# Reordering steps of a hand-written schedule, and moving two small start-up loads from ScalarE's queue to GpSimd's

## The chip, the cores and the metric

One core of a Trainium2 chip runs the whole program. The metric is the device time of one execution in microseconds (us); the kernel before was timed three times. A change of under 0.2%, about 2 us here, can't be told from no change.

## The reference, cut to what matters

Two layers of a hybrid decoder run over a prompt of 512 rows and over a sample group of 8 sequences with 8 new rows each (64 rows) and 2048 past positions.

```python
for l in range(DEPTH):                       # 2 layers; for the prompt rows, then for the sample rows
    h = rmsnorm(x, norm_pre[l]); z = h @ w_in[l]          # 1024 -> 3912 columns
    q, k, v, qi, ki, wi, ga, xb, gb, u, vc, gc = split(z)  # q, k, qi, ki get a partial rotation (rope)
    score = sum_h relu(qi . ki) * wi                      # indexer, causal
    idx = top_k(score)                                    # prompt 128 of 512, sample 256 of 2056
    ya = softmax(q . k[idx]) @ v[idx]                     # sample: keys and values of 16 pages of 128 and 8 new rows
    yb = (trailing window means of xb - xb) @ pool_w * pool_scale
    yc = u * (tril(sgu_w) @ layernorm(vc) + sgu_b)
    y = concat(ya * silu(ga), yb * silu(gb), yc * silu(gc))
    x = x + rmsnorm(y @ w_out[l], norm_post[l])
```

All is float32. The selection is computed as a mask: the kernel finds the threshold of the k-th score and adds minus infinity to what lies below it.

## The kernel before, in words

**Tiles.** The 576 rows are five row tiles: ST (the 64 sample rows) and 0 to 3 (128 prompt rows each). HT holds the normalised, transposed input; a projection step ("z", name, tile) multiplies one row tile by one 512-column chunk of w_in, 8 matmuls (L1573), for the ST tile in two column halves (L1547). A matmul of float32 appears twice in the trace's counts. "zk" is a part of such a step. The results lie in two PSUM banks that ScalarE empties (lines 905 to 931); three other banks are emptied by VectorE. A step that writes a bank waits until its last user is copied out.

**Order.** One list, written by hand in `_order()`, says what comes after what. Each engine's program runs through the same list and emits its own part of every step, so moving an entry moves work on TensorE (PE), ScalarE (ACT) and VectorE (DVE) at once. Both layers use the same list. `filler[m]` holds what is put around the heads 2m and 2m+1 of the prompt attention: its first part before the transposes of the previous pair's weights ("pt", L1932), its second part between those and the previous pair's product with V ("pv", L1831).

**Steps that the change touches.**
- ("snew", p): logits of the new sample keys (L1705). The first one waits for VectorE's copy of the transposed new keys, `pe.wait_ge(dve_free, dve_no(l, "kT", ST) + 1)`, the copy being L1264. Between them stands VectorE's bitwise search for the sample threshold ("sel", L1123 to L1156), then "take" (from L1162 on), which makes the mask.
- ("rope", "k", t), ("T", "kT", t): VectorE rotates the keys of tile t (L1114 to L1117), TensorE transposes them (L1586), VectorE copies them out (L1266). ("psel", a, b) is b - a rounds of VectorE's top-8 search in the prompt scores (L1131, L1134); 16 rounds are needed.
- ("K", p, j), ("V", p, j): TensorE runs over 8 pages of the cache (L1690, L1754), two sets of four. A page is 256 KB. SyncE (SP) issues the page loads (L724) into a ring of four groups of two pages, one group as soon as the one four back is used; so each K or V step uses up the ring, and each half of a step needs two groups. `group()` is the wait.
- ("turn", p, j): transposes of the sample weights (L1733), copied by ScalarE (L1020) for the V step. ("mask", p, n): mask spread (L1719, L1722) and added by VectorE (L1193). ("exp", p): ScalarE, L1011.
- ("pool", t), ("pool w", t): the pooling product (L1795, L1796), the gating product (L1802), then L1812. ("ln scale", t): four VectorE operations, L1324 to L1328. ("gaT", t), ("yT", t): transposes of the gate (L1943) and of the branches (L1950), VectorE's L1319 and L1479. ("qk", n): prompt logits, L1820, which VectorE masks (L1300).

**Start.** SyncE loads x_sample, the page table and the first prompt tile. ScalarE's queue loads the 128 x 128 identity and norm_pre (L944, L945), then, once the fourth part of the first weight chunk is in, the other three prompt tiles (L952). GpSimd (POOL) loads the first chunk of w_in in four parts (L759), the ki columns, the other constants (L798), and half of the indexer keys (L674); SyncE begins its half of the keys after the fourth weight part too. The first transposes (L1848) turn x into HT through L1237. `turn_x(0, 1)`, the transposes of prompt tile 0, stand after the first projection step.

Of the kernel before, what the change touches and what calls it, by code (L numbers as in the profile page):

```python
# [50 lines left out]
ST = PT_TILES  # L51
# [9 lines left out]
ROUNDS = KP // 8  # L61
# [32 lines left out]
CONST = {}  # L94
# [84 lines left out]
def _order():  # L179
    s = []  # L180

    def z(name, *tiles):
        s.extend(("z", name, rt) for rt in tiles)

    def rope(name, *tiles):
        s.extend(("rope", name, rt) for rt in tiles)

    def turned(name, *tiles):
        s.extend(("T", name, rt) for rt in tiles)
# [38 lines left out]
    for n in range(len(SI) + 1):  # L228
# [44 lines left out]
    s.append(("take",))  # L273
    z("v", 0)
    s.append(("snew", 0))
# [44 lines left out]
    z("gc", 0)  # L320
    rope("k", 2, 3)
    turned("kT", 1)
    s.append(("V", 1, 0))
    s += [("turn", 1, 1), ("psel", 9, 11)]
    z("gc", 1)
    turned("kT", 2)
# [4 lines left out]
        0: ([("z", "gc", 3), ("psel", 11, 13)], []),  # L331
        1: ([("z", "uv", ST), ("V", 1, 1), ("turn", 1, 2)], [("z", "uv", 0), ("K", 2, 3), ("psel", 13, 15)]),
        2: ([("zk", "uv", 1, 0, 4)], [("z", "uv", 1), ("V", 1, 2), ("turn", 1, 3), ("psel", 15, ROUNDS), ("pmask",)]),
# [7 lines left out]
        9: ([("gate", 1), ("snew", 3)], [("z", "ga", ST), ("K", 3, 3), ("pool", 1), ("yT", 0), ("pool w", 1), ("ln scale", 2)]),  # L341
        10: ([("ok", 0, 0, 4)], [("V", 2, 2), ("turn", 2, 3), ("gaT", 1), ("mask", 3, 0)]),
        11: ([("o", 0), ("ln scale", 3)], [("V", 2, 3), ("pool", 2), ("mask", 3, 1), ("turn", 2, 4), ("mask", 3, 2), ("exp", 3), ("pool w", 2)]),
# [16 lines left out]


ORDER = _order()


# [102 lines left out]
def build(nc, x_prompt, x_sample, k_pages_t, v_pages_n, kidx_t, state_pool, page_order, norm_pre_t, w_in, pool_w,  # L467
# [4 lines left out]
    with ExitStack() as ctx:  # L472
# [3 lines left out]
        def sem(name):  # L476
            return ctx.enter_context(nc.semaphore(name))
# [28 lines left out]
        V = vt[:, :].rearrange("p (t d) -> p t d", t=5)  # L506
# [43 lines left out]
        cst = sb("cst", consts.shape[1])  # L550
# [33 lines left out]
        gpre = sb("gpre", KC)  # L584
# [19 lines left out]
        gpre_first_in, gpre_in, gpost_in = sem("gpre_first_in"), sem("gpre_in"), sem("gpost_in")  # L604
# [36 lines left out]
        ident_in = sem("identity_in")  # L641
# [37 lines left out]
        n_id = CONST["ident"][1]  # L679
# [58 lines left out]
        def _(pool):  # L738
            def load_w(l, i, first=0, end=4):
# [8 lines left out]
                if i < len(CHUNKS):  # L748
                    _, c0, w = CHUNKS[i]
# [126 lines left out]
        def _(act):  # L876
# [67 lines left out]
            act.dma_start(cst[:, 0:n_id], consts[:, 0:n_id]).then_inc(ident_in, 16)  # L944
            act.dma_start(gpre[:, :], norm_pre_t[0]).then_inc(gpre_first_in, 16)  # L945
# [136 lines left out]
        def _(dve):  # L1082
# [275 lines left out]
            dve.wait_ge(gpre_first_in, 16)  # L1358
# [5 lines left out]
            for l in range(DEPTH):  # L1364
# [127 lines left out]
                for i, rt in enumerate(RTO):  # L1492
# [19 lines left out]
                    if l + 1 < DEPTH and i > 0:  # L1512
                        if i == 1:
                            dve.wait_ge(gpre_in, 16 * (l + 1))
                        if i <= 2:
                            copy_ht(l + 1, RTO[i - 1])
                        norm(l + 1, i - 1)
# [3 lines left out]
        def _(pe):  # L1521
# [356 lines left out]
            turn_x(0, 0)  # L1878
            for l in range(DEPTH):
                for s in ORDER:  # L1880
                    if s[0] == "x":
                        turn_x(l, s[1])
                    elif s[0] == "z":
                        project_tile(l, s[1], s[2], DONE_K.get(s[1:], 0))
                        if l == 0 and s == ORDER[0]:
                            turn_x(0, 1)
# [124 lines left out]
```

## Time and profile before

| | us |
|---|---|
| three runs | 1025.37, 1026.67, 1026.81 |
| median | 1026.67 |
| the profiled execution's own time | 1025.37 |
| its span in the trace | 1023.2 |
| PE busy | 985.8 |
| DVE busy | 564.3 |
| ACT busy | 297.1 |

The span is first to last instruction; 2.2 us of the execution lie around it. Layer 0 fills the time to about 510 us, layer 1 the rest. "Idle before" in a row is the time in which that engine did nothing ahead of the instruction, and the arrow names what released it. Some matmul records are missing, so not each hole between rows is a wait; a bracket with a releaser is.

### The profile page before, as it was taken

Reading aid. Unit: us, or ns where it says so; the run is one execution under the profiler, and the core shown is the slowest. Engines: PE = TensorE matmul, PEld = TensorE weight load, DVE = VectorE, ACT = ScalarE, POOL = GpSimd, SP = SyncE. Lnnn points to the kernel's source line nnn. Section 1 sums busy time; section 2 is a strip of 40 time slices with the busy share of each in tenths; the row PEclk is TensorE's granted clock in tenths of the full one; section 3 lists DMA queues with packets and bytes.
Section 4 is the critical chain, followed back from the end, with each engine's and each line's share of the span. In section 5 each row is a group of like instructions: output and inputs, shape, how many; then the busy total and the mean of one; then the engine's idle time right before and its main releaser. Section 6 shows DMA issues by size and latency. Waiting matters only on the chain.

```text
span 1023.2 us, 18691 instructions
## 1 busy us (share of the span) xinstructions
PE 985.8 (96%) x6442; PEld 503.0 (49%) x6442; DVE 564.3 (55%) x1733; ACT 297.1 (29%) x620; POOL 168.8 (16%) x290
## 2 busy tenths in 40 slices
PE   6999999999899999999999999999999999999994
PEld 4446444444654455555453644434456445555551
DVE  3327998566762345443541699955877324354332
ACT  2321111531331534232322211135123235323231
POOL 8450100110120000002725011010011200000000
PEclk9999999999999999999999999999999999899997
DMA  9382666466885666566542367674779666465521
GB/s 290 75 254 81 229 219 224 181 229 234 292 306 188 218 215 228 185 208 229 173 133 79 111 200 237 224 241 142 250 235 312 239 209 234 145 242 190 202 80 62
DMA packets 107391, 205.28 MB, mean 201 GB/s; under 512 B 15687, under 2 KB 24214, under 8 KB 107298
## 3 DMA queue, kind: packets, MB, share of 16 engines
q1 hardware_dynamic: 87474, 148.68, 42.4%
q0 software_dynamic: 19104, 53.77, 16.9%
q10 hardware_dynamic: 720, 1.64, 0.5%
q8 instruction: 52, 0.85, 0.4%
q14 instruction: 41, 0.34, 0.1%
HBM read 194.00 MB, written 10.14 MB: 200 GB/s over the span
## 4 chain that ended last, share of the span: by engine, by line
PE 89%; DVE 4%; DMA 2%; ACT 2%; SPq 1%; issue 1%; ACTq 0%; DVEq 0%; POOLq 0%
PE bank L1573 41%; PE bank L1871 11%; PE bank L1690 6%; PE bank L1754 6%; PE bank L1547 4%; PE bank L1820 3%; PE bank L1831 2%; PE bank L1906 2%; PE bank L1653 2%; PE bank L1669 2%; PE bank L1932 2%; PE bank L1866 1%; PE bank L1733 1%; DMA pg<-in_cache_v_dram 1%; PE bank L1586 1%; SPq L724 1%
## 5 line engine op out<-in xcount | busy, mean ns | idle before, releaser
L1573 PE MATMUL bank<-wr,ht 128*128 128x512 f32 (+1 forms) x1024 | 439.6, 576 | 3.7 <-ACT za L921 2.4
L1573 PEld LDWEIGHTS bank<-wr,ht 128*128 128x128 f32 x1024 | 187.3, 191 | 204.1 <-issue 194.7
L759 POOL DMA_DIRECT2D wr<-in_w_in_dram x64 | 46.6, 729 | 409.1 <-PE bank L1573 360.9
L1123 DVE TENSOR_SCALAR_CACHE_REDUCE r<-r,sel_i 128x1088 bf16<-128x1088 f32 x62 | 83.5, 1346 | 2.0
L674 POOL DMA_DIRECT2D pg<-in_cache_kidx_dram x128 | 67.0, 529 | 47.9 <-issue 42.1
L1754 PE MATMUL bank<-pg,rs 128*32 128x256 f32 x1024 | 64.2, 390 | 1.5 <-DMA pg<-in_cache_v_dram 1.0
L1690 PE MATMUL bank<-pg,r 128*32 128x256 f32 x1024 | 62.5, 382 | 1.1 <-DMA pg<-in_cache_k_dram 1.0
L759 POOL DMA_DIRECT2D wr<-in_w_out_dram x16 | 11.6, 726 | 294.2 <-PE bank L1871 132.7
L1547 PE MATMUL bank<-wr,ht 128*64 128x256 f32 (+1 forms) x512 | 58.2, 382 | 1.1 <-DMA wr<-in_w_in_dram 1.1
L1871 PE MATMUL bank<-wr,gr 128*128 128x512 f32 x128 | 58.5, 597 | 0.0
L1871 PE MATMUL bank<-wr,ht 128*128 128x512 f32 x128 | 58.3, 598 | 0.0
L1057 ACT ACTIVATE r<-r 128x128 f32<-128x128 f32 (+3 forms) x64 | 35.7, 559 | 63.4 <-DVE r L1303 63.2
L1134 DVE MATCH_REPLACE8 r<-r 128x256 f32<-128x256 f32 (+2 forms) x96 | 51.1, 543 | 0.0
L1300 DVE CUSTOM_DVE_ANT_0 r<-bank,r 128x256 f32<-128x256 f32 (+2 forms) x48 | 26.5, 553 | 42.9 <-PE bank L1820 42.9
L1690 PEld LDWEIGHTS bank<-pg,r 128*32 128x32 f32 x1024 | 29.9, 109 | 37.2 <-issue 18.5
L1754 PEld LDWEIGHTS bank<-pg,rs 128*32 128x32 f32 x1024 | 30.3, 111 | 36.0 <-issue 20.3
L1131 DVE MAX8 r<-r 128x8 f32<-128x256 f32 (+2 forms) x96 | 47.2, 547 | 0.6
L1547 PEld LDWEIGHTS bank<-wr,ht 128*64 128x64 f32 x512 | 35.9, 142 | 22.0 <-issue 6.5
L1020 ACT ACTIVATE rs<-bank 128x512 f32<-128x512 f32 (+1 forms) x40 | 21.1, 529 | 83.9 <-PE bank L1733 70.6
L1402 DVE COPY r<-bank 64x256 f32<-64x256 f32 x16 | 6.8, 422 | 63.0 <-PE bank L1669 62.9
L931 ACT ACTIVATE za<-bank,stats 128x512 f32<-128x512 f32 x16 | 11.0, 688 | 99.4 <-PE bank L1573 99.4
L1004 ACT ACTIVATE sh<-bank 128x512 f32<-128x512 f32 x32 | 19.1, 597 | 70.3 <-PE bank L1690 70.3
(256 smaller groups left out, 1235.3 us busy)
## 6 DMA issues: line engine op xcount, KB each, us to landing
pg<-in_cache_k_dram SPq DMA_DIRECT2D x256, 256.0 KB, 4.3
pg<-in_cache_v_dram SPq DMA_DIRECT2D x256, 256.0 KB, 4.5
wr<-in_w_in_dram POOLq DMA_DIRECT2D x56, 512.0 KB, 4.6
wr<-in_w_out_dram POOLq DMA_DIRECT2D x16, 512.0 KB, 4.5
pg<-in_cache_kidx_dram POOLq DMA_DIRECT2D x128, 32.0 KB, 2.3
pg<-in_cache_kidx_dram SPq DMA_DIRECT2D x128, 32.0 KB, 2.4
r<-in_x_prompt_dram SPq DMA_DIRECT2D x5, 512.0 KB, 6.2
out_dram<-vt POOLq DMA_DIRECT2D x8, 256.0 KB, 4.5
```

Source lines behind the costliest of these rows:

```text
L674: queue.dma_start(PG[2 * (g % 4) + e][par * HD:(par + 1) * HD, c0:c0 + PAGE], kidx_t[l, bass.ds(nos[u * 4 + par * 2 + f], 1), :, :].rearra ...
L759: pool.dma_start(W[n % 2][:, n4 * 2:n4 * 2 + 2, 0:w], src[:, n4 * 2:n4 * 2 + 2, :])\
L1057: nc.scalar.activation(SP_[n % 4][:, 0:w], SP_[n % 4][:, 0:w], ACT.Exp, bias=NB_[:, n:n + 1], scale=HD ** -0.5, accum_out=SM[:, n:n + 1]). ...
L1123: ins = nc.vector.tensor_scalar(junk[i][0:m, 0:part.shape[1]], part, sc, None, ALU.is_ge, ALU.add, accum_out=CNT[0:m, i:i + 1])
L1131: ins = nc.vector.max(BEST[:, i, :], part)
L1134: ins = nc.vector.match_replace(part, BEST[:, i, :], part, TAKEN)
L1547: mm = pe.matmul(b[t * NS:(t + 1) * NS, 0:w // 2], HT[:, k, SEQ:SEQ + NS], weights[:, k, t * (w // 2):(t + 1) * (w // 2)], start=(k == 0), ...
L1573: mm = pe.matmul(b[0:m, 0:w], HT[:, k, rt * P:rt * P + m], weights[k], start=(k == 0), stop=(k == KC - 1), skip_group_check=(k1 - k0 < KC))
L1690: mm = pe.matmul(bk[r0:r0 + HW, u * 256:(u + 1) * 256], QBX[:, 2 * e + k, q0:q0 + HW], two[par][:, :, 2 * e + k, :], start=(k == 0), stop= ...
L1754: mm = pe.matmul(acc[r0:r0 + HW, 0:DP], r[:, c0:c0 + HW], PG[s0[par] + e][:, g * DP:(g + 1) * DP], start=(j == 0 and u == 0 and e == 0), s ...
L1820: pe.matmul(b[:, 0:w], QT[part, h // 2, i * P:(i + 1) * P], KT[part, h // 2, 0:w], start=True, stop=True).then_inc(dve_full, 1)
L1871: mm = pe.matmul(b[0:m, :], y, W[n % 2][:, k, :], start=(i == 0), stop=(i == KC - 1), skip_group_check=(k1 - k0 < KC))
```

## The change

Two kinds of edits. First, `_order()` is altered in ten places, for both layers. Second, the identity and norm_pre loads go from ScalarE's program to the top of GpSimd's, ahead of the first weight chunk, norm_pre now counted on the semaphore that layer 1 also uses, and `turn_x(0, 1)` goes ahead of the first projection step.

```diff
     turned("kT", ST)
-    s.append(("take",))
+    s += [("take",), ("snew", 0)]
     z("v", 0)
-    s.append(("snew", 0))
...
     z("gc", 0)
+    s.append(("V", 1, 0))
+    s += [("turn", 1, 1), ("psel", 9, 11)]
     rope("k", 2, 3)
     turned("kT", 1)
-    s.append(("V", 1, 0))
-    s += [("turn", 1, 1), ("psel", 9, 11)]
     z("gc", 1)
+    s.append(("psel", 11, 12))
     turned("kT", 2)
...
-        0: ([("z", "gc", 3), ("psel", 11, 13)], []),
+        0: ([("z", "gc", 3), ("psel", 12, 14)], []),
...
-        9: ([("gate", 1), ("snew", 3)], [("z", "ga", ST), ("K", 3, 3), ("pool", 1), ("yT", 0), ("pool w", 1), ("ln scale", 2)]),
-        10: ([("ok", 0, 0, 4)], [("V", 2, 2), ("turn", 2, 3), ("gaT", 1), ("mask", 3, 0)]),
-        11: ([("o", 0), ("ln scale", 3)], [("V", 2, 3), ("pool", 2), ("mask", 3, 1), ("turn", 2, 4), ("mask", 3, 2), ("exp", 3), ("pool w", 2)]),
-        12: ([("V", 2, 4), ("od", 2), ("pool", 3)], [("turn", 3, 0), ("yT", 1), ("V", 3, 0), ("pool w", 3), ("ok", 1, 0, 4)]),
-        13: ([("turn", 3, 1), ("o", 1), ("V", 3, 1)], [("yT", 2), ("gate", 2), ("yTs",)]),
-        14: ([("turn", 3, 2)], [("gaT", 2), ("yo", 2), ("yT", 3)]),
-        15: ([("V", 3, 2), ("ok", 2, 0, 4)], [("turn", 3, 3), ("o", 2)]),
+        9: ([("gate", 1), ("snew", 3)], [("K", 3, 3), ("z", "ga", ST), ("pool", 1), ("yT", 0), ("pool w", 1), ("ln scale", 2)]),
+        10: ([("ok", 0, 0, 4)], [("V", 2, 2), ("turn", 2, 3), ("gaT", 1), ("ln scale", 3), ("mask", 3, 0)]),
+        11: ([("o", 0)], [("pool", 2), ("mask", 3, 1), ("V", 2, 3), ("turn", 2, 4), ("mask", 3, 2), ("exp", 3), ("pool w", 2)]),
+        12: ([("V", 2, 4), ("od", 2), ("pool", 3)], [("turn", 3, 0), ("yT", 1), ("pool w", 3), ("V", 3, 0), ("ok", 1, 0, 4)]),
+        13: ([("turn", 3, 1), ("o", 1), ("V", 3, 1), ("yT", 2)], [("gate", 2), ("yTs",)]),
+        14: ([("turn", 3, 2)], [("gaT", 2), ("yo", 2), ("yT", 3), ("V", 3, 2)]),
+        15: ([("ok", 2, 0, 4)], [("turn", 3, 3), ("o", 2)]),
...
         def _(pool):
+            n_id = CONST["ident"][1]
+            pool.dma_start(cst[:, 0:n_id], consts[:, 0:n_id]).then_inc(ident_in, 16)
+            pool.dma_start(gpre[:, :], norm_pre_t[0]).then_inc(gpre_in, 16)
...
-            act.dma_start(cst[:, 0:n_id], consts[:, 0:n_id]).then_inc(ident_in, 16)
-            act.dma_start(gpre[:, :], norm_pre_t[0]).then_inc(gpre_first_in, 16)
...
             turn_x(0, 0)
+            turn_x(0, 1)
             for l in range(DEPTH):
...
-                        if l == 0 and s == ORDER[0]:
-                            turn_x(0, 1)
```

In filler 1 and 2 the last psel rounds go from 13 to 15 and 15 to 16 to 14 to 16 in filler 1 alone; in filler 4 ("K", 3, 0) goes ahead of ("mask", 2, 1). In the new file the lines after 735 stand mostly one to three lower.

TensorE around the first "snew", before: the transposes of the new keys, the v projection of tile 0, then the new keys' logits (small, r), and the next projection part.

```order
L1586 MATMUL bank<-cst,zb 128x64 x4
L1573 MATMUL bank<-wr,ht 128x512 x8
L1705 MATMUL bank<-small,r 32x64 x8
L1573 MATMUL bank<-wr,ht 128x512 x4
L1690 MATMUL bank<-pg,r 32x256 x16
```

The same place in the changed kernel.

```order
L1587 MATMUL bank<-cst,zb 128x64 x4
L1706 MATMUL bank<-small,r 32x64 x8
L1574 MATMUL bank<-wr,ht 128x512 x12
L1691 MATMUL bank<-pg,r 32x256 x16
L1574 MATMUL bank<-wr,ht 128x512 x2
```

The logits now stand directly behind the transposes.

TensorE from the gc projection of the ST tile on, before: the gc projection of tile 0, the transposes of key tile 1 (cst, zb), V step (1, 0) (pg, rs), the weight transposes (cst, sh), gc of tile 1, key tile 2, gc of tile 2, K step (2, 2).

```order
L1547 MATMUL bank<-wr,ht 64x128 x16
L1573 MATMUL bank<-wr,ht 128x256 x8
L1586 MATMUL bank<-cst,zb 128x128 x4
L1754 MATMUL bank<-pg,rs 32x256 x16
L1733 MATMUL bank<-cst,sh 128x128 x4
L1573 MATMUL bank<-wr,ht 128x256 x8
L1586 MATMUL bank<-cst,zb 128x128 x4
L1573 MATMUL bank<-wr,ht 128x256 x8
L1690 MATMUL bank<-pg,r 32x256 x16
```

The same place in the changed kernel.

```order
L1548 MATMUL bank<-wr,ht 64x128 x16
L1574 MATMUL bank<-wr,ht 128x256 x8
L1755 MATMUL bank<-pg,rs 32x256 x16
L1734 MATMUL bank<-cst,sh 128x128 x4
L1587 MATMUL bank<-cst,zb 128x128 x4
L1574 MATMUL bank<-wr,ht 128x256 x8
L1587 MATMUL bank<-cst,zb 128x128 x4
L1574 MATMUL bank<-wr,ht 128x256 x8
L1691 MATMUL bank<-pg,r 32x256 x16
```

The V step and the weight transposes moved ahead of key tile 1. On VectorE two psel rounds now stand between the rotation of key tile 1 and those of tiles 2 and 3, and one round between the copies of key tiles 1 and 2.

TensorE around V step (3, 2), before: the end of the product of a head pair with V (r or pt, vt), the logits of the next pair (kt, qt), the V step, the first part of output tile 2.

```order
L1831 MATMUL bank<-r,vt 64x128
L1831 MATMUL bank<-pt,vt 64x128
L1820 MATMUL bank<-kt,qt 128x512 x2
L1754 MATMUL bank<-pg,rs 32x256 x16
L1871 MATMUL bank<-wr,ht 128x512 x4
```

The same V step in the changed kernel, from the transposes of "yT" 3 (cst, gr) on.

```order
L1950 MATMUL bank<-cst,gr 128x128 x4
L1755 MATMUL bank<-pg,rs 32x256 x16
L1832 MATMUL bank<-r,vt 64x128
L1832 MATMUL bank<-pt,vt 64x128
L1832 MATMUL bank<-r,vt 64x128
```

It now comes ahead of the whole product of the head pair and of the next logits.

## Rows read from the trace of the kernel before

**Rows 1.** Page, part 1: busy us, share, instructions.

```profile
PE 985.8 (96%) x6442; PEld 503.0 (49%) x6442; DVE 564.3 (55%) x1733; ACT 297.1 (29%) x620; POOL 168.8 (16%) x290
```

**Rows 2.** Waits of TensorE: engine line <- releaser: us, times, longest.

```profile
PE bank L1586 <- DVE zb L1117: 4.3, 2, 2.2
...
PE bank L1812 <- DVE sst L1193: 1.8, 2, 0.9
...
PE bank L1690 <- DMA pg<-in_cache_k_dram: 1.0, 1, 1.0
...
PE bank L1722 <- DVE zb L1343: 1.0, 2, 0.5
```

**Rows 3.** Timeline, PE, start: us, duration, what.

```profile
7.13 6.46 PE L1547 MATMUL bank<-wr,ht 128*64 128x256 f32 x32 [1.13 <-DMA wr<-in_w_in_dram]
13.52 1.09 PE L1848 MATMUL bank<-cst,r 128*128 128x128 f32 x8
14.54 1.21 PE L1573 MATMUL bank<-zb,ht 128*64 128x72 f32 x16
18.13 3.70 PE L1573 MATMUL bank<-wr,ht 128*128 128x512 f32 x8 [2.37 <-ACT za L921]
```

**Rows 4.** Timeline, start, other engines.

```profile
6.64 0.56 POOL L798 DMA_DIRECT2D cst<-in_consts_dram  x1
...
7.52 1.06 ACT L940 ACTIVATE gr<-r 128x1024 f32<-128x1024 f32 x1 [0.76 <-DMA r<-in_x_prompt_dram]
...
15.60 1.41 ACTq L952 DMA_DIRECT2D r<-in_x_prompt_dram  x3
```

**Rows 5.** DMA issues, 0 to 22 us: issuer, KB, us to landing.

```profile
cst<-in_consts_dram ACTq DMA_DIRECT2D x1, 64.0 KB, 2.3
```

**Rows 6.** Timeline, PE and DVE, around the first "snew".

```profile
161.10 7.13 PE L1573 MATMUL bank<-wr,ht 128*128 128x512 f32 x16
163.06 0.42 DVE L1264 COPY small<-bank 128x256 f32<-128x256 f32 x1
169.01 0.70 PE L1573 MATMUL bank<-wr,ht 128*128 128x512 f32 x1 [0.40 <-ACT vt L931]
```

**Rows 7.** Timeline, DVE, a psel round, a key copy, a rotation's end.

```profile
260.78 1.48 DVE L1131 MAX8 r<-r 128x8 f32<-128x256 f32 x3
...
264.00 0.69 DVE L1266 COPY kt<-bank 128x512 f32<-128x512 f32 x1
...
266.24 0.29 DVE L1117 TENSOR_TENSOR zb<-zb,plt 128x128 f32<-128x128 f32 x1
```

**Rows 8.** Timeline, DVE, mask and "ln scale" of tile 3.

```profile
405.67 0.68 DVE L1193 CUSTOM_DVE_ANT_0 sh<-sh,bank 128x512 f32<-128x512 f32 x1
...
408.21 0.15 DVE L1324 RECIPROCAL stats<-stats 128x1 f32<-128x1 f32 x1
...
409.19 0.42 DVE L1328 TENSOR_TENSOR gr<-gr,pscale 128x256 f32<-128x256 f32 x1
```

**Rows 9.** Pages of V step (3, 2): issues, us to landing.

```profile
L724 SPq DMA_DIRECT2D pg<-in_cache_v_dram x8: 333/333/1162, 438.8 to 443.6; - x8
...
DMA to landing us min/median/max: 4.7/5.8/6.3
```

**Rows 10.** Chain that ended last, 438 to 452 us: start, us, what.

```profile
440.73 0.69 DVE r L1471
...
441.46 1.09 PE bank L1831 x16
...
447.26 1.02 PE bank L1831 x16
448.28 1.06 PE bank L1820 x4
449.34 1.86 PE bank L1754 x32
```

**Rows 11.** Stretch: length, PE DVE ACT POOL busy, PEclk, DMA share, GB/s.

```profile
764.10:767.50 3.40, 3.40 (x33) 1.57 (x25) 3.33 (x10) 0.00 (x0) 0.00 (x0) 0.55 0.59 193
```

More of the change, by code:

```diff
@@ L330, in _order @@
     filler = {
-        0: ([("z", "gc", 3), ("psel", 11, 13)], []),
-        1: ([("z", "uv", ST), ("V", 1, 1), ("turn", 1, 2)], [("z", "uv", 0), ("K", 2, 3), ("psel", 13, 15)]),
-        2: ([("zk", "uv", 1, 0, 4)], [("z", "uv", 1), ("V", 1, 2), ("turn", 1, 3), ("psel", 15, ROUNDS), ("pmask",)]),
+        0: ([("z", "gc", 3), ("psel", 12, 14)], []),
+        1: ([("z", "uv", ST), ("V", 1, 1), ("turn", 1, 2)], [("z", "uv", 0), ("K", 2, 3), ("psel", 14, ROUNDS)]),
[1 row of a table added]
         3: ([("snew", 2), ("yo", 0), ("zk", "uv", 2, 0, 4)], [("z", "uv", 2), ("V", 1, 3), ("turn", 1, 4)]),
[1 row of a table removed]
[1 row of a table added]
         5: ([("z", "ga", 0)], [("K", 3, 1), ("turn", 2, 0)]),
@@ L603, in build @@
         small_in, table_in = sem("small_in"), sem("table_in")
-        gpre_first_in, gpre_in, gpost_in = sem("gpre_first_in"), sem("gpre_in"), sem("gpost_in")
+        gpre_in, gpost_in = sem("gpre_in"), sem("gpost_in")
         wt_ready = sem("gating_weights_ready")
@@ L678, in build @@
         block = ctx.enter_context(nc.Block())
-        n_id = CONST["ident"][1]
         @block.sync
@@ L1357, in _ @@
             dve.wait_ge(init_done, 1)
-            dve.wait_ge(gpre_first_in, 16)
+            dve.wait_ge(gpre_in, 16)
             for i in range(2):
@@ L1513, in _ @@
                         if i == 1:
-                            dve.wait_ge(gpre_in, 16 * (l + 1))
+                            dve.wait_ge(gpre_in, 16 * (l + 2))
                         if i <= 2:
```

3 rows, old and new, of the table filler are left out of this document.

## The prediction

> **What bounds the kernel now.** I read the page first, then TensorE's waits, then the timelines around each place that the change touches, and for the page loads the landing times. TensorE is busy for 985.8 of 1023.2 us and no other engine for more than 564 [rows 1], so the time is TensorE's queue from end to end, and an edit counts only by what it puts into or takes out of TensorE's waits. These are few and each is small: 4.3 us for the rotated keys (two waits, one a layer), 1.8 and 1.0 us for VectorE ahead of the last mask and of L1812, 1.0 us once for cache pages [rows 2], some microseconds at the start [rows 3]. All the change can gain lies in those; what it can lose is set by how close the other engines stand behind. The work of TensorE itself is not changed by one matmul.
>
> **The start.** The first projection runs from 7.13 to 13.6 us, the transposes of prompt tile 0 take 1.09 behind it, the ki projection 1.2, and then TensorE waits 2.37 us until 18.13 for ScalarE to empty the first bank [rows 3]. ScalarE is late because it first finishes the norm of tile 0, which hangs on those transposes, and then issues three loads for 1.41 us from 15.60 on [rows 4]. With the transposes in front, the norm is long done. The tile is in at 7.5 us [rows 4]; transposes to 8.6, the projection of 6.46 to 15.1, its two copies end at 16.1, the ki projection at 16.3, where tile 0's projection can start: 1.8 us earlier than 18.13. The loads in GpSimd's queue put the weights back by two issues of 0.56 each [rows 4], 1.1 us, which the later start of the projection (8.6 for 7.1) hides. The identity took 2.3 us on ScalarE's queue [rows 5] and now goes through a queue on which no small first load is shown; if it takes 2.3 there too it lands at about 3.7, under the 4.9 at which x_sample lets the first transposes go. Bounds: -2.6 if the projection, which ran at 0.20 us a record here against half of that later in the trace, speeds up where it did, and +0.9 if the identity comes as late as the first weight part did (7.1), which pushes all behind it. I take -1.8, once.
>
> The Trainium skill (DMA: Bandwidth & Descriptors, Specifications and Issuing engine by pattern) speaks against this part: plain loads belong on the sync or scalar queue, with a first byte after about 0.6 us against about 1 us from GpSimd. By that the identity would come 0.4 us later than it did, and the start would still be bound by x_sample. The trace of before has no like pair of loads to check it.
>
> **The first "snew".** TensorE has the new keys transposed at 161.1 and goes into the v projection until 168.2; VectorE copies those keys only at 163.06 to 163.48, because its threshold search stands in front [rows 6]. Nothing in the change moves VectorE's work there, and its chain up to there has no wait for TensorE in it since 92.8 us, so the distance stays. Put directly behind the transposes, the logits wait from 161.15 to 163.5: +2.35 us, and the whole of TensorE's queue waits behind them. Later the projection part behind them need no longer wait 0.40 for ScalarE [rows 6]. Net +1.95 a layer, +3.9 in all. Layer 1 has the same order and the same distance. Bounds +1.5 and +2.1 a layer; below that nothing can go, since the instructions on both engines are the same.
>
> **Key tiles, V step (1, 0) and psel.** The wait of 2.16 us a layer [rows 2] is for the rotation of tile 1, which stands on VectorE behind two psel rounds. The V step and the weight transposes now fill it. But tile 2's rotation comes behind two more rounds. A round is 260.78 to 264.00, 3.2 us; the rotations of tiles 1 and 2 lie between 264.6 and 266.5, 0.95 each [rows 7]. So tile 2 is rotated 2 x 3.2 + 0.95 = 7.35 after tile 1 (at 265.6), at 273.0, and its transposes, which began at 272.2, wait for it: +0.8. What the V step now waits for its own pages, being 2.6 us earlier, ends under this wait. The page wait of 1.0 at the following K step in layer 0 [rows 2] goes, its pages being asked for earlier: -0.4 there with the small parts. In layer 1 TensorE ran V step (1, 0) at half clock [rows 11], 1.6 us that the new wait covers: -0.9. Sum -1.3. Bounds: -5.3 (the wait gone in both layers, and the page wait) and +2.
>
> **"ln scale" 3, "pool" 2, V (2, 3).** VectorE's four operations, 408.21 to 409.61, are put ahead of the mask work at 405.67 [rows 8]. The second of the logits behind needs the bank that the first mask operation frees, now 1.4 later: +1.3. Against it the V step stands between the mask products and what waits for them, and the waits of 0.9 and 0.5 a layer [rows 2] go: -1.4. Net -0.1 in both layers together; bounds -2.8 and +2.6.
>
> **"yT" 2 ahead of the weights' transposes.** The head product at 441.46 waits for VectorE's copies of the transposed weights, the last begun at 440.73 [rows 10]. Ahead of the two now stands one more copy of 0.6: +0.6 a layer, +1.2. Bounds 0 and +1.4.
>
> **V step (3, 2).** It moves ahead of a head product and two logits, 1.02 and 1.06, from 449.34 to 447.2 [rows 10]. Its last two pages are issued up to 443.6 and take 5.8 to land in the median [rows 9]: 449.4. The second half needs them at 448.1, and waits 1.35. What lies behind, head product and output projection, needs as long as before. +2.7 for two layers; bounds 0 (landing after the 4.7 of the quickest) and +3.6 (after the 6.3).
>
> **The rest** (K (3, 3) and K (3, 0) earlier, L1812 ahead of V (3, 0), psel in fillers 1 and 2) exchanges neighbours on TensorE whose inputs are ready by the trace, and costs nothing; K (3, 3), 3.6 us earlier, uses up its margin on pages: 0 to +0.7.
>
> **Sum.** -1.8 + 3.9 - 1.3 - 0.1 + 1.2 + 2.7 = +4.6 us on the profiled execution's 1025.37 (span 1023.2, 2.2 around it). It lies 1.3 under the median of 1026.67; the difference is carried over, which gives 1031.3 us.
>
> **Rivals.**
> (B) The page waits don't come and the start gives its best. For it: landing varies between 4.7 and 6.3 [rows 9]. Against it: the ring allows no earlier issue. 4.6 - 2.7 - 0.8 = +1.1, 1027.8, no change that can be told.
> (C) The clock decides, on the faster side. In 764.1 to 767.5 the granted clock was 0.55 [rows 11], half of 2.4 GHz; just before, TensorE had stood for 2.16 us for tile 1's rotation. By the same view two more such stretches lie at 419.4 (3.4 us) and 869.9 (6.9 us), the first behind the waits for the last mask. Together 13.7 us at half speed, 6.8 lost. If the clock no longer falls once those waits are filled, 5.9 more than I counted come back, and the 1.3 by which the median is above the profiled run too: 1024.1. It decides once three of these falls are gone. Against it: the change makes new waits of 2.35 and 2.
> (D) The reverse: the four new waits (two at "snew", two at tile 2) each bring one such stretch of 3.4 us, 1.7 lost in each: +6.8, 1038. For it: the wait of 2.16 did so in one layer. Against it: in the other it did not.
>
> **Chances.** Forecast 0.56, B 0.19, C 0.13, D 0.12. What can be told from no change is 0.2%, 2.05 us. Slower 0.68 (forecast and D), same 0.19, faster 0.13. The forecast's own range is 1028.7 to 1034; the range that holds 8 in 10 reaches into B and D and the unknown clock: 1025.8 to 1035.5.
>
> **What would show it.** In the changed profile: the new keys' logits begin about 2.3 us behind the transposes, released by VectorE's copy, in both layers; tile 0's first projection part at about 16.3; key tile 2's transposes wait about 2 us for the rotation; a wait for cache_v pages of about 1.4 in V step (3, 2); no waits ahead of the last mask and L1812, but 1.3 at the logits before. It is wrong if the logits find the keys copied, if the V step finds its pages, or if the granted clock falls at other places than before for more than 3 us in all.

## The result, and the profile after

| | before | changed |
|---|---|---|
| first timing, median of 6 runs each | 1026.74 | 1036.53 |
| ratio, 95% interval | | 1.0099 [1.0076, 1.0121] |
| second timing (that of e9 below), median of 27 and 12 runs | 1028.73 | 1033.30 |
| ratio, 95% interval | | 1.0038 [1.0016, 1.0061] |
| profiled execution, its own time | 1025.37 | 1030.69 |
| its span, mean granted clock | 1023.2, 0.988 | 1029.0, 0.994 |

The changed kernel is slower: +9.8 us in the first timing, +4.6 in the second. 1031.3 was forecast from 1026.7, with 1025.8 to 1035.5 as the range. The sign was right, and the first measurement lies outside.

One measure is used below beside the time. The granted clock of TensorE differs from execution to execution: in 125 runs of the kernel before its mean lay anywhere between 0.977 and 0.994, and those runs spread from 1023 to 1036 us. (One further run of it and one each of e7 and e15, over 1.5% above the fastest of their kernels, are left out everywhere.) A "fall" below is a stretch in which the granted clock stands at half. It costs half its length where TensorE is the limit, so **span times mean granted clock** follows what the execution would take without falls ("at equal clock"). Its mean was 1012.5 to 1012.9 for the kernel before in each of the four batches of timings, and it tells single edits apart better than the time does.

Two things in it are not the cost of falls. First, each profile also ends at half clock, with TensorE's last matmul long done; in the kernel before no engine is busy there (columns: stretch, length, busy us of PE, PEld, DVE, ACT, POOL with counts, granted clock, DMA share, GB/s):

```profile
1013.00:1023.20 10.20, 0.00 (x0) 0.00 (x0) 0.00 (x0) 0.00 (x0) 0.00 (x0) 0.50 0.13 50
```

This end lasted 9.0 to 12.2 us in the seventeen profiles, so it takes 4.5 to 6.1 us off each product and cancels in a difference only to about 1 us. Second, 1.7 us of a timed execution lie around the span where the two loads are moved, and 2.1 elsewhere. Taken of the whole time, such a kernel is 0.4 better than the column "equal clock" below says: e1 -1.9, e14 +0.8, e9 +7.7, e10 +4.5, e11 -2.2, e12 -4.5.

The two profiles differ by 5.8 us in span (5.3 in time), but the kernel before lost 6.8 us to three falls of the clock ahead of its end and the changed one 1.7 to this one (columns as above):

```profile
910.70:914.10 3.40, 3.40 (x6) 1.28 (x5) 1.36 (x8) 1.42 (x4) 0.00 (x0) 0.51 0.71 244
```

With these falls taken out, the changed profile is 10.9 us longer.

TensorE's work is the same; part 1 of the changed kernel's page, against [rows 1], is 2.4 us less busy; less of it ran at half clock:

```profile
PE 983.4 (96%) x6442; PEld 502.6 (49%) x6442; DVE 563.8 (55%) x1733; ACT 297.2 (29%) x620; POOL 169.2 (16%) x292
```

The waits of TensorE in the changed kernel, against [rows 2]:

```profile
PE bank L1755 <- DMA pg<-in_cache_v_dram: 6.8, 10, 1.3
PE bank L1706 <- DVE small L1265: 4.7, 2, 2.4
...
PE bank L1587 <- DVE zb L1118: 3.8, 2, 2.0
PE bank L1821 <- DVE sst L1194: 2.8, 4, 1.0
PE bank L1832 <- DVE r L1472: 1.4, 2, 0.7
...
PE bank L1813 <- DVE r L1472: 0.8, 2, 0.5
...
PE bank L1691 <- DMA pg<-in_cache_k_dram: 0.7, 1, 0.7
```

The waits ahead of the last mask and of L1812 are gone as forecast, and so is the one for ScalarE at the start. New are the one for the new keys (4.7), ten waits for V pages where there were two of 1.0 in all, four for VectorE's mask operation, two at the head product and two at a pooling product.

A wait printed there is not all that was lost: a group whose instructions wait for one another shows its first wait and grows longer. So each instruction of TensorE was set against the same one of the kernel before (the n-th of its line and tiles), and the shift read at both ends of each edit's place. The ledger of these shifts, in us, has the falls of the clock taken out. It is that of one pair of executions:

| place | forecast | layer 0 | layer 1 |
|---|---|---|---|
| start | -1.8 | -2.6 | |
| first snew | +3.9 | +1.9 | +1.9 |
| V (1, 0), psel, key tiles | -1.3 (+0.4 without the clock) | -0.3 | +1.2 |
| K (3, 0) ahead of mask (2, 1) | 0 | +1.1 | +1.1 |
| K (3, 3) ahead of ga | 0 to +0.7 | +0.8 | 0 |
| ln scale 3, pool 2, V (2, 3) | -0.1 | -0.2 | -0.1 |
| pool w 3 ahead of V (3, 0) | 0 | +0.9 | +1.2 |
| yT 2 ahead of pt | +1.2 | +0.7 | +0.7 |
| V (3, 2) | +2.7 | +0.9 | +1.6 |

The rows sum to 10.8; page waits at other places, up to 0.6 each and of both signs, nearly cancel. Two rows that were forecast at nothing, K (3, 0) and pool w 3, make 4.3 of it.

**Start.** TensorE in the changed kernel, against [rows 3]. Columns: start, duration, engine, line, what, idle before and its releaser.

```profile
4.69 1.11 PE L1849 MATMUL bank<-cst,r 64*128 64x64 f32 x8 [4.69 <-DMA cst<-in_consts_dram]
6.80 1.97 PE L1849 MATMUL bank<-cst,r 128*128 128x128 f32 x8 [1.00 <-DMA r<-in_x_prompt_dram]
8.71 5.79 PE L1548 MATMUL bank<-wr,ht 128*64 128x256 f32 x32
14.33 1.16 PE L1574 MATMUL bank<-zb,ht 128*64 128x72 f32 x16
15.55 3.70 PE L1574 MATMUL bank<-wr,ht 128*128 128x512 f32 x8
```

Tile 0's projection starts at 15.55 for 18.13. The identity's load was issued later (at 1.40 for 0.88) and took 3.3 us for the 2.3 of [rows 5], so it landed at about 4.7 and not at the 3.7 of the prediction. It now is what the first transposes wait for; they start no later, since x_sample had held them until 4.91. On GpSimd's slower first byte the Trainium skill (DMA: Bandwidth & Descriptors, Specifications) and the trace agree in the direction: the page has about 1 us against about 0.6, and here the same load took 1.0 us more from issue to landing.

**First snew.** As forecast, in both layers:

```profile
158.14 0.46 PE L1587 MATMUL bank<-cst,zb 64*128 64x64 f32 x4
160.94 0.45 PE L1706 MATMUL bank<-small,r 128*32 128x64 f32 x16 [2.34 <-DVE small L1265]
161.31 8.85 PE L1574 MATMUL bank<-wr,ht 128*128 128x512 f32 x20
```

**V step (1, 0) and the key tiles.** Layer 0:

```profile
263.33 1.07 PE L1755 MATMUL bank<-pg,rs 128*32 128x256 f32 x16
265.56 1.07 PE L1755 MATMUL bank<-pg,rs 128*32 128x256 f32 x16 [1.16 <-DMA pg<-in_cache_v_dram]
266.56 0.66 PE L1734 MATMUL bank<-cst,sh 128*128 128x128 f32 x4
267.05 0.60 PE L1587 MATMUL bank<-cst,zb 128*128 128x128 f32 x4
267.49 3.62 PE L1574 MATMUL bank<-wr,ht 128*128 128x256 f32 x16
272.93 0.63 PE L1587 MATMUL bank<-cst,zb 128*128 128x128 f32 x4 [1.82 <-DVE zb L1118]
```

The key wait of 2.16 is gone. In its place are 1.16 for pages in the V step and 1.82 for the rotation of tile 2.

**K (3, 0) ahead of mask (2, 1).** First the kernel before, then the changed one: the mask product and the K step in their two orders (in the second only the end of the K step), and the logits of the next head pair.

```profile
331.00 0.40 PE L1719 MATMUL bank<-r,repb 64*128 64x256 bf16 x4
331.33 1.93 PE L1690 MATMUL bank<-pg,r 128*32 128x256 f32 x32
...
333.69 0.70 PE L1820 MATMUL bank<-kt,qt 64*128 64x256 f32 x4
```

```profile
331.75 1.05 PE L1691 MATMUL bank<-pg,r 128*32 128x256 f32 x16
332.73 0.40 PE L1720 MATMUL bank<-r,repb 64*128 64x256 bf16 x4
...
333.91 1.30 PE L1821 MATMUL bank<-kt,qt 64*128 64x256 f32 x4 [0.39 <-DVE sst L1194]
```

The mask product now stands behind the K step, so VectorE adds the mask, and frees the bank, later. Its first mask operation, before and then changed:

```profile
331.43 0.69 DVE L1193 CUSTOM_DVE_ANT_0 sh<-sh,bank 128x512 f32<-128x512 f32 x1 [2.85 <-PE bank L1719]
```

```profile
333.16 0.69 DVE L1194 CUSTOM_DVE_ANT_0 sh<-sh,bank 128x512 f32<-128x512 f32 x1 [4.72 <-PE bank L1723]
```

The logits wait 0.39 at their start and lengthen from 0.70 to 1.30, about 1 us in all, in both layers.

**pool w 3 and V (3, 0)**, and then **the head product behind yT 2** and **V (3, 2)**, all in layer 0:

```profile
426.05 0.68 PE L1813 MATMUL bank<-pw,plt 128*128 128x128 f32 x4 [0.36 <-DVE r L1472]
426.66 1.07 PE L1755 MATMUL bank<-pg,rs 128*32 128x256 f32 x16
428.18 1.07 PE L1755 MATMUL bank<-pg,rs 128*32 128x256 f32 x16 [0.45 <-DMA pg<-in_cache_v_dram]
...
443.20 0.32 PE L1832 MATMUL bank<-kip,vt 128*64 128x128 f32 x1 [0.71 <-DVE r L1472]
...
448.92 1.07 PE L1755 MATMUL bank<-pg,rs 128*32 128x256 f32 x16
450.70 1.07 PE L1755 MATMUL bank<-pg,rs 128*32 128x256 f32 x16 [0.72 <-DMA pg<-in_cache_v_dram]
```

### The profile page after: what moved, and what is told of

It reads as the page before. It is cut to its first block, busy times and chain, and to the rows that moved or that the text cites. A ratio compares the mean times of both kernels' runs of the same rounds, so it can differ in the third digit from the quotient of the medians.

```text
span 1029.0 us, 18691 instructions
## 1 busy us (share of the span) xinstructions
PE 983.4 (96%) x6442; PEld 502.6 (49%) x6442; DVE 563.8 (55%) x1733; ACT 297.2 (29%) x620; POOL 169.2 (16%) x292
## 4 chain that ended last, share of the span: by engine, by line
PE 69%; DVE 18%; DMA 6%; SPq 3%; issue 2%; ACT 2%; DVEq 0%
PE bank L1574 29%; PE bank L1872 11%; DVE r L1124 8%; DMA pg<-in_cache_v_dram 5%; PE bank L1755 4%; PE bank L1691 3%; SPq L723 3%; PE bank L1548 3%; PE bank L1821 2%; PE bank L1654 2%; PE bank L1670 2%; PE bank L1906 2%; DVE sel_i L1155 2%; PE bank L1832 1%; PE bank L1867 1%
## 5 line engine op out<-in xcount | busy, mean ns | idle before, releaser
L1429 DVE SCALAR_TENSOR_TENSOR r<-rs,wi,r 128x256 f32<-128x256 f32 (+2 forms) x42 | 26.0, 618 | 24.0 <-ACT rs L998 21.5
```

## The experiments

Fifteen kernels, in four batches, each batch on one chip beside 27 to 35 runs of the kernel before. "Median" is that of the timed runs (12, where no other number stands), "equal clock" the difference to the kernel before in mean span times clock with its 95% interval, "clock" the mean granted clock (that of the kernel before behind it). Kernels of one batch are set against the same runs of the kernel before, so they share its error: e1 to e4, e5 to e8, e9 to e12, e13 to e15.

| | median / before | ratio [95%] | equal clock | clock / before |
|---|---|---|---|---|
| e1 start | 1026.6 / 1029.9 | 0.9969 [0.9948, 0.9989] | -1.5 ± 1.8 | 0.987 / 0.985 |
| e2 snew | 1036.5 / 1029.9 | 1.0058 [1.0031, 1.0084] | +3.6 ± 1.4 | 0.982 / 0.985 |
| e3 keys | 1028.6 / 1029.9 | 0.9972 [0.9943, 1.0002] | -1.5 ± 1.3 | 0.985 / 0.985 |
| e4 mask | 1029.3 / 1029.9 | 1.0008 [0.9980, 1.0035] | +1.7 ± 1.4 | 0.987 / 0.985 |
| e5 lnpool | 1028.7 / 1029.9 | 0.9993 [0.9967, 1.0018] | +2.1 ± 1.5 | 0.988 / 0.985 |
| e6 poolw | 1028.3 / 1029.9 | 0.9982 [0.9959, 1.0006] | +1.8 ± 1.3 | 0.988 / 0.985 |
| e7 yT 2 (11 runs) | 1027.8 / 1029.9 | 0.9976 [0.9947, 1.0006] | +2.0 ± 1.3 | 0.989 / 0.985 |
| e8 V (3, 2) | 1032.1 / 1029.9 | 1.0015 [0.9988, 1.0042] | +3.1 ± 1.2 | 0.986 / 0.985 |
| e9 changed, again | 1033.3 / 1028.7 | 1.0038 [1.0016, 1.0061] | +8.1 ± 1.2 | 0.989 / 0.985 |
| e10 no snew | 1028.3 / 1028.7 | 0.9986 [0.9962, 1.0010] | +4.9 ± 1.3 | 0.991 / 0.985 |
| e11 start, keys (10 runs) | 1022.1 / 1028.7 | 0.9939 [0.9916, 0.9963] | -1.8 ± 1.0 | 0.990 / 0.985 |
| e12 start, V first (6 runs) | 1020.2 / 1028.7 | 0.9898 [0.9867, 0.9929] | -4.1 ± 1.4 | 0.991 / 0.985 |
| e13 transposes | 1025.6 / 1028.0 | 0.9975 [0.9954, 0.9997] | -2.7 ± 1.4 | 0.987 / 0.987 |
| e14 loads | 1028.9 / 1028.0 | 1.0016 [0.9988, 1.0043] | +1.2 ± 1.6 | 0.987 / 0.987 |
| e15 K (3, 3) (11 runs) | 1030.7 / 1028.0 | 0.9998 [0.9973, 1.0023] | -0.6 ± 1.5 | 0.986 / 0.987 |

**e1, the start alone, and its halves e13 and e14.** e1 makes the edits of the change at L944, L945 and at `turn_x`; e13 moves `turn_x(0, 1)` alone, e14 the loads alone.

```diff
+            turn_x(0, 1)
-                        if l == 0 and s == ORDER[0]:
-                            turn_x(0, 1)
+            pool.dma_start(cst[:, 0:n_id], consts[:, 0:n_id]).then_inc(ident_in, 16)
+            pool.dma_start(gpre[:, :], norm_pre_t[0]).then_inc(gpre_in, 16)
```

> The kernel before with the start of the changed one alone (identity and norm_pre through GpSimd's queue, tile 0's transposes ahead of the first projection). Theory A (an edit costs the waits at its own place, the granted clock takes no side): the first projection part of tile 0 begins at about 15.6 us for 18.13, and all of it is kept to the end: -2.6 us. Theory B (the timed loss of 9.8 us, 4.5 more than between the two profiled executions, comes from more falls of the clock): also about -2.6 here, since no wait is added. Theory C (what TensorE gains it gives back at the cache pages, which do not come earlier): -1.2 or less, with new page waits of 0.4 or more in layer 0.

> The kernel before with the transposes of prompt tile 0 alone ahead of the first projection; identity and norm_pre stay on ScalarE's queue. A: all of the start's gain is in the transposes, tile 0's first projection part begins 1.5 to 2.5 us earlier than 18.13, -2 us by time multiplied by clock. Forecast of the start: -1.8, of which this is all. Rival: the transposes are only worth something with the loads moved, 0 to -0.5.

> The kernel before with the identity and norm_pre loads alone moved to GpSimd's queue ahead of the first weight chunk. A: the weights come two issues of 0.56 us later and the first projection with them, +1.1 us; ScalarE, free earlier, doesn't change the wait for the first bank. Rival: 0 or a small gain, since the first projection also waits for the transposes of x_sample, whose identity comes no later.

The start is 3.3 us faster in the times and 1.5 at equal clock; the halves give -2.7 and +1.2 (of the whole time -2.7 and +0.8, e1 -1.9), which add up to it. The transposes carry the gain. What the moved loads do is inside the noise, and by e14's trace it is small: TensorE begins the first projection at 7.62 (7.13 before) and tile 0's projection at 18.44 (18.13 before), and the wait for ScalarE stands as it was. Behind it is a fall of the clock, read off the duration: 5.40 us for the eight products that take 3.70 in [rows 3].

```profile
7.62 6.09 PE L1548 MATMUL bank<-wr,ht 128*64 128x256 f32 x32 [1.81 <-DMA wr<-in_w_in_dram]
...
18.44 5.40 PE L1574 MATMUL bank<-wr,ht 128*128 128x512 f32 x8 [2.57 <-ACT za L924]
```

In e13 the same part has no wait and its full speed:

```profile
8.75 1.97 PE L1848 MATMUL bank<-cst,r 128*128 128x128 f32 x8 [2.46 <-DMA r<-in_x_prompt_dram]
10.65 5.17 PE L1547 MATMUL bank<-wr,ht 128*64 128x256 f32 x32
15.65 1.16 PE L1573 MATMUL bank<-zb,ht 128*64 128x72 f32 x16
16.88 3.70 PE L1573 MATMUL bank<-wr,ht 128*128 128x512 f32 x8
```

Of the ten profiled kernels with that wait nine show this fall (the kernel before, in the execution of [rows 3], is the tenth), of the seven without it none. e1's profile also speaks against theory C: the K step's page wait of 1.0 in layer 0 was 0.2, and two V steps waited 2.0 together. The intervals don't part A from C (-2.6 from -1.2).

**e2, the first snew alone.**

```diff
-    s.append(("take",))
+    s += [("take",), ("snew", 0)]
     z("v", 0)
-    s.append(("snew", 0))
```

> The kernel before with the first snew alone directly behind the transposes of the new keys. A: +1.95 a layer less small change behind, +3.7 us in all. B: as A, and a fall of the clock of 3.4 us behind each of the two waits, +7.1. C: the later page steps find their pages sooner, so that of the 1.95 of each layer less than 1 is left, +2 or less.

+3.6 at equal clock, theory A's number, and +6.6 in the times, close to B's. Both are right: the wait costs what was forecast, and the times add the clock. Theory C's 2 lies below the interval of the 3.6. The fall behind it comes in some executions only: of the six snew waits in the profiles of e2, the changed kernel and e9, three have it. e9's, with the wait just ahead (columns as above; the stretch behind the wait, then the one that holds it):

```profile
163.50:167.00 3.50, 3.50 (x5) 1.35 (x4) 3.42 (x5) 0.05 (x1) 0.00 (x0) 0.52 1.03 386
160.00:163.50 3.50, 1.12 (x25) 0.86 (x22) 3.30 (x9) 0.77 (x2) 0.00 (x0) 1.00 0.95 304
```

**e3, V step (1, 0) and psel ahead of the key tiles, alone.** The edit is that of the change at `rope("k", 2, 3)`, with the three fillers' psel numbers.

> The kernel before with V step (1, 0), its weight transposes and the psel rounds alone ahead of key tiles 1 to 3. A: per layer 2.16 gone, 1.8 to 2.0 new at key tile 2, 1.0 to 1.2 new for pages in the V step; in layer 0 the 1.0 at K step (2, 2) goes: +1 us in all at equal clock. B: +1, and less 1.7 if the fall of the clock behind the old wait in layer 1 goes. What was forecast for this edit: -1.3.

```profile
267.15 1.07 PE L1755 MATMUL bank<-pg,rs 128*32 128x256 f32 x16 [1.16 <-DMA pg<-in_cache_v_dram]
...
274.52 0.63 PE L1587 MATMUL bank<-cst,zb 128*128 128x128 f32 x4 [1.82 <-DVE zb L1118]
```

The two new waits are those of the changed kernel to a hundredth, as theory A has it, yet the sum is -1.5 ± 1.3 and not +1. One thing that A had too small is the page wait at K step (2, 2). It was 1.0 in the kernel before, once; over the eleven profiled kernels that lack this edit it came in 8 of 22 layers, 0.2 to 3.3 us, 15.6 in all, which is 1.4 an execution. In the five kernels with the edit it came in none of 10. One profile shows such a wait at one of its values, not at its mean. This moves A's +1 to about +0.6 only, and the rest of the difference isn't explained. From e11 less e1 the edit comes out at -0.3 ± 2 instead.

**e4, K step (3, 0) ahead of mask (2, 1).**

```diff
-        ... ("mask", 2, 1), ("K", 3, 0), ("od", 1), ...
+        ... ("K", 3, 0), ("mask", 2, 1), ("od", 1), ...
```

> The kernel before with K step (3, 0) alone ahead of the second mask part of group 2. A: the logits of the next head pair wait for the bank that VectorE frees later, as the changed kernel's trace has it: +1.05 us a layer, +2.1 in all. Forecast: nothing (neighbours with ready inputs). B: as A, with no further fall, since the wait is short.

+1.7 ± 1.4 at equal clock, with A's +2.1 inside and the forecast's 0 just outside; no clear change in the time. The trace has the wait and the stretched logits exactly as in the changed kernel, in both layers:

```profile
336.68 1.30 PE L1820 MATMUL bank<-kt,qt 64*128 64x256 f32 x4 [0.39 <-DVE sst L1193]
```

**e5, ln scale 3 and pool 2 alone.** The edits of the change in fillers 10 and 11.

> The kernel before with ln scale 3 alone ahead of the last masks, and pool 2 and the second mask product ahead of V step (2, 3). Theory A (waits at the place, as the changed kernel's trace has them): +1.4 a layer at the logits behind, -1.4 a layer at the two waits that V step (2, 3) now covers, 0 in all. Theory B (clock): the falls of the clock at about 419 and 870 to 920 stood behind those two waits; without the waits they are gone and 1.7 to 3.4 us come back. Theory C (pages): V step (2, 3), now later, finds its pages and V step (2, 4) behind it does not: +0.5 to +1.

+2.1 ± 1.5 at equal clock, nothing in the time. The profile has +1.3 and -1.4 at the two places, as theory A says; what stands beside that is a page wait of 3.3 at K step (2, 2), which is 130 us ahead of the edit and not its doing. Theory B is half right: the fall at 419 is gone, and the one in layer 1 came all the same at 915, behind the new wait of 1.0 at the logits. The interval leaves out theory A's 0, but the trace has no cost at the place, so whether the edit costs anything is left open by this run.

**e6, pool w 3 ahead of V step (3, 0).**

```diff
-        12: (..., ("V", 3, 0), ("pool w", 3), ("ok", 1, 0, 4)]),
+        12: (..., ("pool w", 3), ("V", 3, 0), ("ok", 1, 0, 4)]),
```

> The kernel before with pool w 3 alone ahead of V step (3, 0). A: the last pooling product now waits 0.4 for VectorE's copy (L1471), and V step (3, 0) behind it, being no later than before against its pages, 0.4 to 0.7 in its second half: +0.9 to +1.2 a layer, +2 in all. Forecast: nothing. C: the V step waits for its pages wherever it stands, so that only the 0.4 counts, +0.8.

+1.8 ± 1.3 at equal clock. Here the V step found its pages and only the pooling product waited:

```profile
431.41 0.68 PE L1812 MATMUL bank<-pw,plt 128*128 128x128 f32 x4 [0.36 <-DVE r L1471]
432.02 1.93 PE L1754 MATMUL bank<-pg,rs 128*32 128x256 f32 x32
```

By the trace the edit alone costs 0.4 to 0.5 a layer, which is C's +0.8; the interval holds both C's and A's number. The page wait of 0.45 and 0.73 that the changed kernel's profile has at this V step came neither here nor in the profiles of e9 and e10, which have the edit together with its neighbours. It is one execution's, and not a cost that the edit always brings.

**e7, yT 2 alone.** `("yT", 2)` at the end of filler 13's first part.

> The kernel before with yT 2 alone ahead of the transposes of the weights. A and forecast: the head product behind waits 0.6 to 0.7 more for VectorE's copies, +1.3 in all. C: V step (3, 2) behind it, which is later by that, finds its pages as before; nothing is given back, +1.3 too. Rival: the 0.7 is hidden at the output projection, 0.

The head product waits 0.7 in each layer, and +2.0 ± 1.3 holds the 1.3 expected. The rival's 0 lies outside.

**e8, V step (3, 2) alone.** `("V", 3, 2)` from the head of filler 15 to the end of filler 14.

> The kernel before with V step (3, 2) alone moved ahead of the head product. A and forecast: its second half waits 1.0 to 1.5 for its pages in each layer, +2 to +3 in all. Rival: landing nearer to the quickest 4.7 us, the wait is under 0.5 a layer: +1 or less. B: two more waits of over 1 us, each with a fall of the clock of 3.4 us behind it: +5.5.

+3.1 ± 1.2 at equal clock: the forecast of 2.7 holds. In layer 1 the step waited 0.70 for pages and nothing fell behind it, so B is half right at most. In layer 0 it waited 0.45 and 1.53, and the second half runs at half clock (1.94 for 1.07), the clock having fallen behind the wait:

```profile
456.13 1.07 PE L1754 MATMUL bank<-pg,rs 128*32 128x256 f32 x16 [0.45 <-DMA pg<-in_cache_v_dram]
458.73 1.94 PE L1754 MATMUL bank<-pg,rs 128*32 128x256 f32 x16 [1.53 <-DMA pg<-in_cache_v_dram]
```

**e15, K step (3, 3) alone.**

```diff
-        9: (..., [("z", "ga", ST), ("K", 3, 3), ...
+        9: (..., [("K", 3, 3), ("z", "ga", ST), ...
```

> The kernel before with K step (3, 3) alone ahead of the ga projection of the sample tile. A: its second half waits 0.6 to 0.8 us for pages in one layer or both, +0.7 to +1.5 by time multiplied by clock. Forecast: 0 to +0.7. Rival: its margin of 3.3 us on the pages covers the 3.6 it moves, 0.

-0.6 ± 1.5, and no page wait at the step in either layer: the rival holds. The changed kernel waited 0.66 there in layer 0, e9 and e10 0.40 each, so the wait seems to need the other edits.

**e9, the changed kernel again, and e10, the same without the snew edit.**

> The changed kernel again, beside runs of the kernel before on the same chip, so that it can be set against the single edits. Theory A (the loss is the sum of the waits of its edits): time multiplied by the granted clock lies 9 to 10 us above the kernel before, the sum of the eight single edits by that measure being 10.2. Rival (the edits disturb each other): it lies above by 13 or more, or by less than 7. Clock as in the kernel before within 0.002.

> The changed kernel with the first snew alone put back behind the v projection of tile 0. A: 3.5 to 3.9 us faster than the changed kernel. B (clock): 6 to 7 faster, as its single edit cost in the times. C (pages): with TensorE 1.9 a layer earlier, page waits grow by 0.5 to 1 a layer, and only 2 to 2.5 come back.

At equal clock the changed kernel is 8.1 ± 1.2 above the kernel before; the nine single edits sum to 10.7, with an interval of about ± 4. The 8.1 is below the 9 to 10 of theory A and above the 7 of the rival, with both just inside the interval; no disturbance of one edit by another is needed, and none is excluded. The expectation for the clock (within 0.002 of the kernel before) was missed: it was 0.989 for 0.985, 3.4 us of 1030, and so the times show only +4.6. Without snew 3.2 ± 1.3 come back at equal clock and 5.0 in the medians: theory A's wait, and the clock on top. C's 2 to 2.5 lies inside that interval too, but the page waits of e10's profile are not longer than those of e9's (4.2 and 0.6 us for V and K pages, against 5.7 and 0.4).

**e11, the start and the key edit together, and e12, a version of our own.** e12 takes the start, and moves V step (1, 0) ahead of key tile 1 as the change does, but leaves the rotations ahead of the psel rounds:

```diff
     rope("k", 2, 3)
+    s += [("V", 1, 0), ("turn", 1, 1)]
     turned("kT", 1)
-    s.append(("V", 1, 0))
-    s += [("turn", 1, 1), ("psel", 9, 11)]
+    s.append(("psel", 9, 11))
     z("gc", 1)
```

> The kernel before with two edits of the change alone: the start, and V step (1, 0) with the psel rounds ahead of the key tiles. A: the sum of the two singles, -2.8 us by time multiplied by clock, faster than both kernels. C (pages give it back): -1.3, the start alone.

> The kernel before with the start of the changed one, and V step (1, 0) and its weight transposes put ahead of the transposes of key tile 1, but with the rotations of key tiles 2 and 3 left ahead of the psel rounds. A: the wait of 2.16 us a layer is filled, 1.2 a layer comes new for pages in the V step, the 1.9 a layer at key tile 2 does not come, and the page wait at K step (2, 2) goes: 1.9 a layer better than start_keys, -5 to -6 us against the kernel before. Rival (the transposes of key tile 1, now later, hold up its copy and with it the logits): no better than start_keys.

Both beat both kernels. e11's -1.8 ± 1.0 at equal clock holds A's -2.8 and C's -1.3 alike; the rest of its 6.6 us in the medians is a clock of 0.990 for 0.985. e12 is at 0.9898 [0.9867, 0.9929] of the kernel before, 8.5 us, of which 4.1 ± 1.4 at equal clock, for the 5 to 6 expected. Its timeline shows the page wait in the V step and none at the key tiles:

```profile
261.12 1.07 PE L1755 MATMUL bank<-pg,rs 128*32 128x256 f32 x16
263.44 1.07 PE L1755 MATMUL bank<-pg,rs 128*32 128x256 f32 x16 [1.26 <-DMA pg<-in_cache_v_dram]
...
264.94 0.60 PE L1587 MATMUL bank<-cst,zb 128*128 128x128 f32 x4
265.38 3.62 PE L1574 MATMUL bank<-wr,ht 128*128 128x256 f32 x16
268.83 0.60 PE L1587 MATMUL bank<-cst,zb 128*128 128x128 f32 x4
```

It is 2.3 ± 1.7 better than e11 at equal clock, where 3.8 was expected. K step (2, 2) in layer 1 had its page wait again (1.5), so the key edit's other gain may be partly lost here.

## Why the prediction was wrong

**Right, in mechanism and size.** The snew wait (+3.9 forecast, +3.7 in the ledger, +3.6 in e2), ln scale and pool 2 in the ledger (-0.1, -0.3), yT 2 (+1.2, +1.4), V (3, 2) (+2.7, +2.5; e8 +3.1). The start has the right mechanism and was set too small: -1.8 for -2.6. The prompt tile was in at 6.8 and not at 7.5; the transposes took 1.97 us for the 1.09 I took, but the projection behind them 5.79 for 6.46. The sum also kept 2.2 us around the span, which is 1.7 in the changed kernel.

**The step that failed** is "the rest exchanges neighbours on TensorE whose inputs are ready by the trace, and costs nothing". K (3, 0) lost nothing itself, but the mask product that it passed came 1.7 us later (332.73 for 331.00), VectorE's mask work with it, and the logits behind need the bank which that work frees: 2.2 in both layers together, with the same wait of 0.39 a layer in the profiles of e4, e9 and e10. I had asked this question of ln scale 3, where the answer was right, and not here. For pool w 3 the input was in fact not ready: VectorE's copy had been covered by the 1.93 of the V step in front, and came 0.36 and 0.46 late without it, 0.8, in every profile with the edit. The other 1.2 of that row are page waits of the V step behind, which the profiles of e9 and e10 don't have. So the step that was put at nothing costs 3 us each time, and 4.3 in the profiled execution; e4 and e6 together have +3.5 at equal clock.

**The key edit** was nearly right by its waits: tile 2's transposes forecast at 273.0 and measured at 272.93, in a kernel that stood 0.2 us earlier just ahead of the place. Up to there +0.8 a layer was forecast, and the shifts are +0.9 in layer 0 and +1.2 in layer 1; in layer 0 the page wait at K step (2, 2) goes, as forecast, which makes the -0.3 of the ledger. That wait was counted at the one value that one profile showed; its mean is 1.4 an execution for that 1.0. By e3 the edit is even a gain, -1.5 ± 1.3; by e11 less e1 it is -0.3 ± 2.

**The clock.** Rivals C and D were both true in part. Old waits had falls behind them: at the start 9 of 10, at key tile 1 14 of 22 over all profiled kernels. New waits have them too: snew 3 of 6, key tile 2 2 of 10. A third pair is the largest: the old waits of 0.49 and 0.88 us ahead of the last mask and of L1812 had a fall behind them in 19 of 26 layers, four of these falls 13.7 us long, and the wait of 1.01 at the logits, which took their place, in 5 of 8. By these shares and lengths, an estimate, the old waits cost an execution 7.8 us of clock and the new ones 5.0. The change takes away more falls than it adds, and so the second timing gives it back 3.4 us of its 8.1. The forecast of +4.6 agrees with that second timing (+4.6), and this is no merit: it had 6.2 at equal clock (4.6 and the 1.6 that it took back from the clock at V step (1, 0)) instead of 8 to 11, and 1.6 of clock given back instead of 3.4. Two errors offset.

**What stays open.** Why the first timing shows 9.8 and the second 4.6: the intervals, 1.0076 to 1.0121 and 1.0016 to 1.0061, don't meet. At equal clock the changed kernel was 1021.9 in the first and 1020.9 in the second, and its mean clock was 0.987 and 0.989, so 2 of the 3.2 us by which its own time differs are clock. The other 2.0 of the 5.2 lie with the kernel before, whose clock in the six runs of the first timing isn't known except for one (0.988). That it was granted a better clock there is likely, not shown. Nor is it shown why key tile 2's wait of 1.6 to 2.5 us brings a fall so much more seldom than key tile 1's 2.16 or the shorter waits ahead of L1812.

## What to carry to other kernels

When a step is moved, ask of each step that it passes what that one releases, and follow this to the next bank or buffer in demand: K (3, 0) cost 2.2 us that way with none of its own inputs late. Where two waits stand one behind the other on the same engine, put work into the first without delaying what ends the second: e12, with the rotations left in front, is 2.3 ± 1.7 us at equal clock better than e11, which has the change's own order there. Weigh small edits by a measure that the clock hardly moves (span times granted clock), and read a page wait over several executions before it is counted as a gain or a loss.

## What the runs showed of the hardware

A wait of TensorE of 2.2 to 2.7 us can cost more than itself: behind it the granted clock falls to half, mostly for 3.4 us, 1.7 more. The fall comes at the same wait in one execution and not in another: 9 of 10, 14 of 22, 3 of 6, 2 of 10 at the four places with waits of about 2 us. The length of the wait doesn't decide it: waits of 0.49 and 0.88 us in a row had one in 19 of 26 layers, and four of these falls lasted 13.7 us, 6.8 lost. This is e8's (the columns of the clock rows above):

```profile
421.30:434.90 13.60, 13.31 (x82) 9.41 (x86) 7.26 (x27) 4.64 (x9) 0.00 (x0) 0.50 0.25 92
```

On this the Trainium skill (TensorE: Matmul & The Clock Gate, What's actually happening) says that the chip's measuring of activity runs freely and isn't reset by a kernel; that the same wait meets it differently each time would fit, and no run here tells it apart. Falls also came where TensorE shows no wait in the 8 us ahead: at 870 to 880 us in four profiles (6.8 us long in the kernel before, e2 and e5, 3.4 in e3), and at about 372 us in e8 and e10.

The mean clock of one kernel varies between executions by 0.004 (standard deviation over the runs of the kernel before), which is 4 us of 1030, more than most of these edits. The wait for page loads at one and the same place, K step (2, 2), varied from nothing to 3.3 us between executions.
